# Table matmuls on TensorE ahead of five stages of a diffusion-transformer layer

## The chip, the cores and the metric

The kernel runs on one core of a Trainium2 chip. The metric is the device time of one execution in microseconds (us), median of several runs. The core's engines are TensorE (PE in the profile; its weight loads are PEld), VectorE (DVE), ScalarE (ACT), GpSimd (POOL) and SyncE (SP, which only issues transfers here).

## What is computed

The reference is one layer (depth 1, batch 1, 2048 latent tokens, 256 context tokens, width 1024, float32) of a hybrid backbone:

```python
h  = rmsnorm(x, norm1_w) * (1 + sc1) + sh1          # sc, sh, gt: silu(c) @ w_mod + b_mod
hc = rmsnorm(ctx, norm1_w) * (1 + csc1) + csh1
# mixer: p = h @ w_in, split into the inputs of three token mixers and 3 x 1024 gate columns
o_a = gdn_out(gdn_bidir(...))      # gated delta rule, 4 heads of 128, both directions, short conv, rotary
o_b = fourier_mix(ub)              # real part of a 2-D DFT over positions and channels
o_c = na_latent(...)               # neighbourhood attention on the latent grid plus context keys
y   = sigmoid(g_a)*(o_a @ w_br_a) + sigmoid(g_b)*(o_b @ w_br_b) + sigmoid(g_c)*(o_c @ w_br_c)
x   = x + gt1 * (y @ w_out)
h2  = rmsnorm(x, norm2_w) * (1 + sc2) + sh2
# 16 experts, each takes its 256 best tokens by router affinity (softmax, top_k)
hid = silu(xe @ w_gate) * (xe @ w_up)
x   = x + gt2 * scatter_add((hid @ w_down) * affinity)
```

## The kernel before

The program is a row of stages, each a function with its own SBUF and PSUM tensors, semaphores and one block of code for each engine: `delta_inputs` (modulation, norm, projection to q, k, v with conv, rotary and transposes), `mixer` (the other projections, Fourier mixing, attention), `delta_rule` (the chunked scan in both directions, written out as steps), `merge` (gates, branch projections, weighted sum), `project_out` (output projection, residual, second norm, router logits), `choose` (the top 256 tokens of each expert) and `experts`. Between two stages stands a barrier of all engines (`Scope.clear` and the end of a block): no engine issues an instruction of the next stage before all have ended the one before, last stores to DRAM included.

Within a stage each engine runs its own list in program order, and semaphores tie the lists together; there is no scheduler or planner. So a matmul stands where the code of TensorE's block puts it, and everything behind it on TensorE waits until it is issued.

Most of the large products are written as three matmuls of the type fp32r: each factor is split into a high part (rounded by ScalarE, `ACT.Copy` into an fp32r tensor) and a low part (the rest, subtracted by VectorE), and high x high, high x low and low x high are added up in PSUM. In `mixer` these are lines 913 to 915, in `merge` 2281 to 2283 (`product`), in `project_out` 2573 to 2575, in `experts` 2970, 2973 and 2987. TensorE can start on a weight tile only when VectorE has made its low part (`sb_wx_low` L1312, `sb_wm_low` L2430, `sb_yp_low` L2661, `sb_xe_parts` L3067). Other products are plain float32 matmuls, among them lines 965 to 968 and the sums of squares, which multiply by the constant table of ones (L2272 in `merge`), and transposes by the identity (L2959 in `experts`, L2584 in `project_out`).

The first work of TensorE behind each barrier that the change touches:

- `mixer`: `project`, 24 matmuls of 128x256 for one weight tile and 256 tokens (L913 to L915), the first one once `sb_wx_low` of weight tile 0 is there.
- `delta_rule`: `keys` and `scores` of both directions (L1780), which wait for the transfers of q and k, then `turn_m` (L1785), which waits for `sb_mt` (VectorE, from POOL's `sb_dq`, L1602).
- `merge`: for block 0, tile 0, `gate` 0 and `gate` 1 (24 matmuls of 128x512 each, whose operands were split in the stage before), then `sums` (4 float32 matmuls L2272 on squares of the two scans' sum, each answered by ACT L2332), then `gate` 2, whose weights ACT splits only behind the four roots L2332.
- `project_out`: `project(0, 0)`, 8 groups of 3 matmuls (L2573 to L2575), which waits for `sb_yp_low`.
- `experts`: `turn(0, 0)`, 16 transposes of the gathered tokens (L2959), then the gate and up products of expert 0.

The constant tables lie in the SBUF tensor `consts_sb`, float32: from column 0 on the identity, a table of ones, a block table and the rotary pairing, 128 columns each.

The functions that the diff touches:

Of the kernel before, what the change touches and what calls it, by code (L numbers as in the profile page):

```python
# [21 lines left out]
P = 128  # L22
# [623 lines left out]
def mixer(nc, g):  # L646
# [80 lines left out]
    with Scope(nc) as c:  # L727
# [15 lines left out]
        bank = psum(nc, c, "mix_ps", (P, 8, 512))  # L743
# [59 lines left out]
        with nc.Block() as block:  # L803
# [89 lines left out]
            def _(pe):  # L893
# [150 lines left out]
                    last.then_inc(sf.pq, 1)  # L1044

                item = 0
                for j, (_, ns) in enumerate(ALL):
                    if j >= NBA:
                        for a in range(CHB):
                            tokens(j, a)  # L1050
                    for t, n in enumerate(ns):
                        project(j, t, n)
                        if item:
                            norm_sum(item - 1)
                        if j >= NBA:
                            item += 1
# [359 lines left out]
def delta_rule(nc, g):  # L1416
# [15 lines left out]
    with Scope(nc) as c:  # L1432
# [66 lines left out]
        with nc.Block() as block:  # L1499
# [274 lines left out]
            def _(pe):  # L1774
# [124 lines left out]
                def step(n, u, old, new):  # L1899
# [74 lines left out]
                        turn_m(1, n + 1, v)  # L1974
                    known(1, n, u, every)
                    second(1, n, u, 6)
                for d in range(2):
                    keys(d, 0, 0, every)
                    scores(d, 0, 0, every)
                    turn_m(d, 0, 0)  # L1980
# [9 lines left out]
            def _(dve):  # L1990
# [116 lines left out]
                for d in range(2):  # L2107
                    matrix(d, 0, 0)
                    begin(d, 0, 0)
                    begin_turns(d, 0, 0)  # L2110
                walk(nc.vector, step)


def late_data(t, lev):
# [10 lines left out]
def merge(nc, g):  # L2125
# [11 lines left out]
    with Scope(nc) as c:  # L2137
# [53 lines left out]
        with nc.Block() as block:  # L2191
# [70 lines left out]
            def _(pe):  # L2262
# [23 lines left out]
                def block(b, more):  # L2286
                    def gate(m, br, first):
                        pe.wait_ge(s.wl, NC * m + br + 1 + WL0)
                        pe.wait_ge(s.sig, NBR * m + br + 1)
                        product(pg[br], br, (hh, hl), range(KD), s.hl if first and br == 0 else None, b).then_inc(s.gate, 1)  # L2290

                    def tile(m, u, first, near, last):
                        start = isinstance(m, int) and m == 0
                        ahead = first or near == 1
                        if ahead:

                            gate(m, 0, first)
                            gate(m, 1, first)
                            if start:
                                sums(0, range(H))  # L2300
                            gate(m, 2, first)
                        for br in order(m):
                            if not ahead:
                                gate(m, br, first)
                            if br == order(m)[0]:
                                pe.wait_ge(s.wl, NC * m + WB + 1 + WL0)
                            pe.wait_ge(s.prod, used(m, br))
                            product(pbr[br], WB, (oh, ol), range(*BRANCH[br]), s.ol if first else None, b).then_inc(s.br, 1)
                            if near == 0 and br < 2:
                                sums(b + 1, (2 * br, 2 * br + 1))  # L2310
                    tiles(nc.tensor, b, more, tile)
                blocks(nc.tensor, block)

            @block.scalar
# [173 lines left out]
def project_out(nc, g):  # L2488
# [4 lines left out]
    with Scope(nc) as c:  # L2493
# [32 lines left out]
        with nc.Block() as block:  # L2526
# [37 lines left out]
            def _(pe):  # L2564
# [31 lines left out]
                def step(t, u, more):  # L2596
# [3 lines left out]
                    project(t, u, 1, False)  # L2600
                    if not first(t):
                        turn(t - 1, 1 - u)
                steps(nc.tensor, step)
                route(LT - 2)
                turn(LT - 1, (LT - 1) % 2)
# [268 lines left out]
def experts(nc, g):  # L2874
# [9 lines left out]
    with Scope(nc) as c:  # L2884
# [17 lines left out]
        with nc.Block() as block:  # L2902
# [48 lines left out]
            def _(pe):  # L2951
# [10 lines left out]
                def expert(e, u, last_one):  # L2962
# [35 lines left out]
                    if last_one:  # L2998
                        last.then_inc(s.front, 1)
                        for f in range(NF):  # L3000
                            down(f, 1).then_inc(s.used, 1)
                turn(0, 0)
                with nc.tensor.Fori(0, E // 2 - 1) as i:
                    for u in range(2):
# [260 lines left out]
def program(nc, g, stages=99):  # L3265

    with Scope(nc) as c:
        consts = sbuf(nc, c, "consts_sb", [P, C_W])
        eps = sbuf(nc, c, "eps_sb", [P, 1])
        g.eps = eps[:]  # L3270
        g.ident, g.ones, g.blk, g.rot = (consts[:, at:at + P] for at in (C_ID, C_ONE, C_BLK, C_ROT))
        g.window = consts[:, C_WIN:C_WIN + GRID]
        g.flip = consts[:, C_FLIP:C_FLIP + P]
        g.dirt = lambda d, j: consts[:, C_DIR + (d * N_DIRT + j) * P:C_DIR + (d * N_DIRT + j + 1) * P]
# [58 lines left out]
```

## Time and profile before

| | |
|---|---|
| time, median of 3 runs | 3819.79 us (3817.61 to 3826.88) |
| span of the profiled execution, first to last instruction | 3823.5 us |
| its mean granted TensorE clock | 0.977 |
| TensorE busy | 3659.4 us, 96% of the span, 19520 matmul records |
| VectorE, ScalarE, GpSimd busy | 2323.0, 1645.7, 856.0 us |
| borders in the trace (us from the start) | mixer 551, delta rule 1157, merge 1661, output projection 2399, experts 2706 |

The profiled execution has no time of its own beside its span; its span lies 3.7 us above the median of the three timed runs and inside their range, so what lies around the span cannot be told from it. The granted clock is a share of TensorE's full 2.4 GHz; 0.50 is 1.2 GHz. A float32 matmul leaves two records in the trace, an fp32r one leaves one.

### The profile page before, as it was taken

Reading aid. Unit: us, or ns where it says so; the run is one execution under the profiler, and the core shown is the slowest. Engines: PE = TensorE matmul, PEld = TensorE weight load, DVE = VectorE, ACT = ScalarE, POOL = GpSimd, SP = SyncE. Lnnn points to the kernel's source line nnn. Section 1 sums busy time; section 2 is a strip of 40 time slices with the busy share of each in tenths; the row PEclk is TensorE's granted clock in tenths of the full one; section 3 lists DMA queues with packets and bytes.
Section 4 is the critical chain, followed back from the end, with each engine's and each line's share of the span. In section 5 each row is a group of like instructions: output and inputs, shape, how many; then the busy total and the mean of one; then the engine's idle time right before and its main releaser. Section 6 shows DMA issues by size and latency. Waiting matters only on the chain. (4 is left out here: it accounts for less than half of the span.)

```text
span 3823.5 us, 58042 instructions
## 1 busy us (share of the span) xinstructions
PE 3659.4 (96%) x19520; PEld 2936.9 (77%) x19520; DVE 2323.0 (61%) x3546; ACT 1645.7 (43%) x3006; POOL 856.0 (22%) x812
## 2 busy tenths in 40 slices
PE   8999999999997999989999999996799999999998
PEld 3444459986777999968888888785688888888887
DVE  4655632555656999953534353444767777677775
ACT  4333333334654666642424332322344445444452
POOL 3888500011106666610000000000000010000100
PEclk9999999999999999989999999997899999999999
DMA  7455455131115433344535352443477676766763
GB/s 283 155 144 142 119 182 130 57 86 45 26 46 183 125 118 122 96 160 125 177 105 170 99 172 73 152 154 130 145 214 226 214 220 206 214 224 215 219 209 92
DMA packets 258768, 570.97 MB, mean 149 GB/s; under 512 B 38971, under 2 KB 117339, under 8 KB 256347
## 3 DMA queue, kind: packets, MB, share of 16 engines
q1 hardware_dynamic: 225612, 451.18, 37.2%
q0 software_dynamic: 33040, 118.25, 10.4%
q8 instruction: 72, 1.18, 0.1%
q14 instruction: 44, 0.36, 0.0%
HBM read 458.27 MB, written 100.73 MB: 146 GB/s over the span
## 5 line engine op out<-in xcount | busy, mean ns | idle before, releaser
L3072 DVE TENSOR_TENSOR sb_we_low<-sb_we,sb_we_high 128x1024 fp32r<-128x1024 f32 x384 | 466.6, 1223 | 121.5 <-ACT sb_we_high L3023 121.5
L3023 ACT ACTIVATE sb_we_high<-sb_we 128x1024 fp32r<-128x1024 f32 x377 | 392.2, 1048 | 142.3 <-PE ey L2987 142.3
L2430 DVE TENSOR_TENSOR sb_wm_low<-sb_wm,sb_wm_high 128x1024 fp32r<-128x1024 f32 x127 | 155.4, 1224 | 393.6 <-ACT sb_wm_high L2340 393.6
L344 PE MATMUL p_ps<-sb_hT,sb_ring 128*128 128x512 f32 (+1 forms) x960 | 373.2, 549 | 0.0
L344 PEld LDWEIGHTS p_ps<-sb_hT,sb_ring 128*128 128x128 f32 x960 | 181.9, 190 | 186.2 <-issue 181.3
L2281 PE MATMUL pg<-sb_hb_high,sb_wm_high 128*128 128x512 f32 x768 | 303.3, 395 | 8.7 <-DVEq L2402 4.6
L2282 PE MATMUL pg<-sb_hb_low,sb_wm_high 128*128 128x512 f32 x768 | 300.4, 391 | 0.0
L2283 PE MATMUL pg<-sb_hb_high,sb_wm_low 128*128 128x512 f32 x768 | 300.1, 391 | 0.0
L2970 PE MATMUL eg<-sb_xe_parts,sb_we_high 128*128 128x512 f32 x1024 | 260.5, 396 | 1.6 <-DVE sb_xe_parts L3067 1.6
L2970 PE MATMUL eu<-sb_xe_parts,sb_we_high 128*128 128x512 f32 x1024 | 259.1, 395 | 0.0
L2932 POOL DMA_INDIRECT out<-sb_ybe,sb_ti x32 | 51.0, 1595 | 880.7 <-DVE sb_ybe L3107 822.7
L1997 DVE STREAM_TRANSPOSE sb_tm<-sb_um 64x128 f32<-64x128 f32 x720 | 219.8, 305 | 13.5
L2368 ACT ACTIVATE sb_sg<-pg 128x512 f32<-128x512 f32 x96 | 57.1, 595 | 396.3 <-PE pg L2283 396.2
L2970 PEld LDWEIGHTS eg<-sb_xe_parts,sb_we_high 128*128 128x128 f32 x1024 | 184.0, 188 | 37.4 <-issue 2.0
L2970 PEld LDWEIGHTS eu<-sb_xe_parts,sb_we_high 128*128 128x128 f32 x1024 | 182.9, 188 | 34.3
L3028 ACT ACTIVATE sb_sge<-sb_sge 128x256 f32<-128x256 f32 x128 | 53.5, 418 | 294.2 <-DVE sb_sge L3078 294.2
L1692 ACT ACTIVATE sb_pm<-dr_first 64x128 f32<-64x128 f32 x432 | 116.9, 271 | 141.0 <-PE dr_first L1798 134.8
L2281 PEld LDWEIGHTS pg<-sb_hb_high,sb_wm_high 128*128 128x128 f32 x768 | 145.0, 189 | 42.2 <-DVE sb_wm_low L2430 6.1
L3080 DVE TENSOR_REDUCE sb_sue<-eu 128x256 f32<-128x512 f32 x128 | 88.5, 692 | 144.8 <-PE eu L2973 143.9
L2282 PEld LDWEIGHTS pg<-sb_hb_low,sb_wm_high 128*128 128x128 f32 x768 | 145.1, 189 | 31.7 <-issue 1.4
L2283 PEld LDWEIGHTS pg<-sb_hb_high,sb_wm_low 128*128 128x128 f32 x768 | 145.2, 189 | 30.3
L2987 PE MATMUL ey<-sb_we_high,sb_hid_low 128*128 128x512 f32 x512 | 159.5, 393 | 0.0
(418 smaller groups left out, 8675.7 us busy)
## 6 DMA issues: line engine op xcount, KB each, us to landing
sb_we<-in_w_ex SPq DMA_DIRECT2D x384, 512.0 KB, 4.5
sb_wm<-in_w_gates SPq DMA_DIRECT2D x96, 512.0 KB, 3.6
sb_stage<-in_w_mod_row POOLq DMA_DIRECT2D x64, 256.0 KB, 3.6
sb_stage<-h_d SPq DMA_DIRECT2D x32, 512.0 KB, 4.3
sb_wm<-in_w_br SPq DMA_DIRECT2D x32, 512.0 KB
sb_ring<-in_w_ch POOLq DMA_DIRECT2D x19, 512.0 KB, 5.2
sb_gr<-gc_d SPq DMA_DIRECT2D x36, 256.0 KB, 3.8
sb_lk<-k_d SPq DMA_DIRECT2D x36, 256.0 KB, 4.0
```

The lines of the kernel that those rows point to most:

```text
L344: last = nc.tensor.matmul(ps[:, b % BANKS, 0:wd], w[:, kind, k], hT[:, k, t0:t0 + wd], start=(k == 0), stop=(k == KD - 1))
L1692: a(pm[d][rows, :, h], pairs(firsts[d])[rows, :, h], ACT.Copy).then_inc(q.pe, 1)
L1997: last = v.transpose(blocks(tm[d][u])[ROWS2[h], :, half], by_head(um[d][u])[ROWS2[half], :, h, half])
L2281: nc.tensor.matmul(bank[:], high, rh[:, k], start=(k == ks[0]), stop=False)
L2282: nc.tensor.matmul(bank[:], high, rl[:, k], start=False, stop=False)
L2283: last = nc.tensor.matmul(bank[:], low, rh[:, k], start=False, stop=(k == ks[-1]))
L2430: v.tensor_tensor(wl[n], w[n], wh[n], ALU.subtract).then_inc(s.wl, 1)
L2970: nc.tensor.matmul(bank[:], wh[:, n % CUT, k * P:(k + 1) * P], both, start=(k == 0), stop=False)
L2987: last = nc.tensor.matmul(py[a][q][:], lhs, rhs[:, n % CUT, q * 512:(q + 1) * 512], start=(f == 0 and lhs is high and rhs is wh), stop=(f ...
L3023: nc.scalar.activation(wh[:, n % CUT], w[:, n % RAW], ACT.Copy).then_inc(s.wh, 1)
L3072: v.tensor_tensor(wl[:, n % CUT], w[:, n % RAW], wh[:, n % CUT], ALU.subtract).then_inc(s.wl, 1)
L3080: v.tensor_reduce(su[:, f % 2], pu[f % 2][:].rearrange("p (a t) -> p t a", a=2), AX_X, ALU.add).then_inc(s.usum, 1)
```

## The change

A helper `keep_warm(nc, bank, tab, times)` issues float32 matmuls of `g.tables` (the first 512 columns of `consts_sb`; its first 128 columns, the identity, are the stationary side) into a PSUM bank that nothing reads before it is written anew. None of them waits for a semaphore or sets one. There are 35 of this size: 5 at the start of TensorE's block in `mixer`, 2 + 1 + 1 in `delta_rule`, 4 at the start of `merge`, 3 before and 2 behind its first `sums` (only for tile 0), 9 at the start of `project_out`, 9 at the start of `experts`. In `delta_rule` four matmuls of 64 rows and 512 columns (`firsts`, `seconds`) and eight of 128 rows, 64 output rows and 128 columns (`b_val`) stand between them. Nothing is removed, and no other engine's list changes.

```diff
--- before.py
+++ after.py
@@ -1044,6 +1044,7 @@
                     last.then_inc(sf.pq, 1)
 
                 item = 0
+                keep_warm(nc, bank[:, 4], g.tables, 5)
                 for j, (_, ns) in enumerate(ALL):
                     if j >= NBA:
                         for a in range(CHB):
@@ -1974,6 +1975,16 @@
                         turn_m(1, n + 1, v)
                     known(1, n, u, every)
                     second(1, n, u, 6)
+                half = slice(HALF, P)
+                keep_warm(nc, flat(b_state), g.tables, 2)
+                for _ in range(2):
+                    mm(flat(firsts[0]), g.tables[0:HALF, 0:P], g.tables[0:HALF, 0:512], start=True, stop=True)
+                    mm(flat(seconds[0]), g.tables[half, 0:P], g.tables[half, 0:512], start=True, stop=True)
+                keep_warm(nc, flat(b_state), g.tables, 1)
+                for _ in range(4):
+                    mm(flat(b_val)[0:HALF, 0:P], g.tables[:, 0:HALF], g.tables[:, 0:P], start=True, stop=True)
+                    mm(flat(b_val)[half, 0:P], g.tables[:, half], g.tables[:, P:2 * P], start=True, stop=True)
+                keep_warm(nc, flat(b_state), g.tables, 1)
                 for d in range(2):
                     keys(d, 0, 0, every)
                     scores(d, 0, 0, every)
@@ -2111,6 +2122,12 @@
                 walk(nc.vector, step)
 
 
+def keep_warm(nc, bank, tab, times):
+
+    for _ in range(times):
+        nc.tensor.matmul(bank, tab[:, 0:P], tab[:, 0:512], start=True, stop=True)
+
+
 def late_data(t, lev):
 
     return t.rearrange("p h (q z) -> p h q z", z=1 << lev)
@@ -2297,7 +2314,9 @@
                             gate(m, 0, first)
                             gate(m, 1, first)
                             if start:
+                                keep_warm(nc, pbr[0][:], g.tables, 3)
                                 sums(0, range(H))
+                                keep_warm(nc, pbr[1][:], g.tables, 2)
                             gate(m, 2, first)
                         for br in order(m):
                             if not ahead:
@@ -2309,6 +2328,7 @@
                             if near == 0 and br < 2:
                                 sums(b + 1, (2 * br, 2 * br + 1))
                     tiles(nc.tensor, b, more, tile)
+                keep_warm(nc, pbr[2][:], g.tables, 4)
                 blocks(nc.tensor, block)
 
             @block.scalar
@@ -2600,6 +2620,7 @@
                     project(t, u, 1, False)
                     if not first(t):
                         turn(t - 1, 1 - u)
+                keep_warm(nc, po[1][0][:], g.tables, 9)
                 steps(nc.tensor, step)
                 route(LT - 2)
                 turn(LT - 1, (LT - 1) % 2)
@@ -2999,6 +3020,7 @@
                         last.then_inc(s.front, 1)
                         for f in range(NF):
                             down(f, 1).then_inc(s.used, 1)
+                keep_warm(nc, pu[1][:], g.tables, 9)
                 turn(0, 0)
                 with nc.tensor.Fori(0, E // 2 - 1) as i:
                     for u in range(2):
@@ -3269,6 +3291,7 @@
         eps = sbuf(nc, c, "eps_sb", [P, 1])
         g.eps = eps[:]
         g.ident, g.ones, g.blk, g.rot = (consts[:, at:at + P] for at in (C_ID, C_ONE, C_BLK, C_ROT))
+        g.tables = consts[:, 0:512]
         g.window = consts[:, C_WIN:C_WIN + GRID]
         g.flip = consts[:, C_FLIP:C_FLIP + P]
         g.dirt = lambda d, j: consts[:, C_DIR + (d * N_DIRT + j) * P:C_DIR + (d * N_DIRT + j + 1) * P]
```

What moves on TensorE, in the program's order. At the start of `project_out` (`po00`, `po10` are PSUM banks of the output projection, `sb_wm0_high` and the like the split w_out, `sb_yp_high` the split rows), before:

```order
L2283 MATMUL pbr2<-sb_obr_high,sb_wm3_low 128x512
L2191 UNCONDITIONAL_BRANCH
L2563 UNCONDITIONAL_BRANCH [waits barrier_Pool_Activation_PE_DVE_SP_release]
L2573 MATMUL po00<-sb_wm0_high,sb_yp_high 128x512 [waits di_conv]
L2574 MATMUL po00<-sb_wm0_low,sb_yp_high 128x512
L2575 MATMUL po00<-sb_wm0_high,sb_yp_low 128x512
```

and now:

```order
L2300 MATMUL pbr2<-sb_obr_high,sb_wm3_low 128x512
L2208 UNCONDITIONAL_BRANCH
L2583 UNCONDITIONAL_BRANCH [waits barrier_Pool_Activation_PE_DVE_SP_release]
L2128 MATMUL po10<-sb_consts_sb 128x512 x9
L2593 MATMUL po00<-sb_wm0_high,sb_yp_high 128x512 [waits di_conv]
L2594 MATMUL po00<-sb_wm0_low,sb_yp_high 128x512
L2595 MATMUL po00<-sb_wm0_high,sb_yp_low 128x512
```

The nine stand behind the barrier's release and ahead of the first real matmul; they are in no other engine's way, but the real one is issued only after them. At the start of `merge` (`pg0`, `pbr2` are banks for a gate and for a branch), now:

```order
L1500 UNCONDITIONAL_BRANCH
L2278 UNCONDITIONAL_BRANCH [waits barrier_Pool_Activation_PE_DVE_SP_release]
L2128 MATMUL pbr2<-sb_consts_sb 128x512 x4
L2298 MATMUL pg0<-sb_hb_high,sb_wm0_high 128x512 [waits di_cdone,di_rot,di_proj]
L2299 MATMUL pg0<-sb_hb_low,sb_wm0_high 128x512
L2300 MATMUL pg0<-sb_hb_high,sb_wm0_low 128x512
```

Before, the first row behind the branch was the matmul into `pg0`; four table matmuls now stand ahead of it. Further on in `merge`, between gate 1 and gate 2 (`pnm` are the banks of the sums of squares), before:

```order
L2281 MATMUL pg1<-sb_hb_high,sb_wm1_high 128x512
L2282 MATMUL pg1<-sb_hb_low,sb_wm1_high 128x512
L2283 MATMUL pg1<-sb_hb_high,sb_wm1_low 128x512
L2272 MATMUL pnm0<-sb_prm,sb_consts_sb 128x512 [waits di_root]
L2272 MATMUL pnm1<-sb_prm,sb_consts_sb 128x512 [waits di_root]
L2272 MATMUL pnm0<-sb_prm,sb_consts_sb 128x512 [waits di_nrm,di_root]
L2272 MATMUL pnm1<-sb_yTb,sb_consts_sb 128x512 [waits di_nrm,di_root]
L2281 MATMUL pg2<-sb_hb_high,sb_wm2_high 128x512 [waits di_rot,di_proj]
L2282 MATMUL pg2<-sb_hb_low,sb_wm2_high 128x512
L2283 MATMUL pg2<-sb_hb_high,sb_wm2_low 128x512
```

and now:

```order
L2298 MATMUL pg1<-sb_hb_high,sb_wm1_high 128x512
L2299 MATMUL pg1<-sb_hb_low,sb_wm1_high 128x512
L2300 MATMUL pg1<-sb_hb_high,sb_wm1_low 128x512
L2128 MATMUL pbr0<-sb_consts_sb 128x512 x3
L2289 MATMUL pnm0<-sb_prm,sb_consts_sb 128x512 [waits di_root]
L2289 MATMUL pnm1<-sb_prm,sb_consts_sb 128x512 [waits di_root]
L2289 MATMUL pnm0<-sb_prm,sb_consts_sb 128x512 [waits di_nrm,di_root]
L2289 MATMUL pnm1<-sb_yTb,sb_consts_sb 128x512 [waits di_nrm,di_root]
L2128 MATMUL pbr1<-sb_consts_sb 128x512 x2
L2298 MATMUL pg2<-sb_hb_high,sb_wm2_high 128x512 [waits di_rot,di_proj]
L2299 MATMUL pg2<-sb_hb_low,sb_wm2_high 128x512
L2300 MATMUL pg2<-sb_hb_high,sb_wm2_low 128x512
```

Three table matmuls now stand between the last matmul of gate 1 and the first sum, and two between the last sum and gate 2.

## Rows read from the trace of the kernel before

**Rows 1.** Windows inside four stages: us, busy us (records) by engine, PEclk, DMA share, GB/s

```profile
570.00:780.00 210.00, 210.00 (x1697) 208.71 (x1695) 94.14 (x82) 81.12 (x168) 5.40 (x8) 1.00 0.36 95
1710.00:2385.00 675.00, 673.05 (x2945) 552.24 (x2944) 288.08 (x330) 236.70 (x298) 32.02 (x53) 1.00 0.42 137
2410.00:2610.00 200.00, 200.00 (x1047) 170.33 (x1045) 94.16 (x105) 53.92 (x101) 14.92 (x28) 1.00 0.41 144
2720.00:3790.00 1070.00, 1070.00 (x5793) 918.57 (x5792) 785.65 (x1037) 511.94 (x699) 77.61 (x59) 1.00 0.68 210
```

**Rows 2.** Windows at the five borders where the granted clock is 0.50, same columns

```profile
553.80:560.50 6.70, 5.97 (x28) 5.98 (x29) 4.17 (x4) 2.17 (x3) 1.59 (x3) 0.50 0.99 317
1158.00:1171.50 13.50, 4.42 (x19) 4.13 (x20) 1.35 (x4) 1.26 (x2) 9.39 (x14) 0.50 1.01 337
1659.80:1666.50 6.70, 4.68 (x11) 3.75 (x12) 0.00 (x0) 0.78 (x1) 2.96 (x4) 0.50 0.52 173
2397.00:2407.20 10.20, 6.06 (x14) 4.78 (x15) 7.34 (x7) 7.68 (x8) 0.00 (x0) 0.50 0.71 250
2704.20:2717.80 13.60, 3.65 (x16) 3.27 (x16) 10.11 (x15) 1.79 (x3) 3.07 (x2) 0.50 0.47 142
```

**Rows 3.** Timeline, float32 matmuls of 512 columns: start, us, engine, line, tiles, records

```profile
867.97 1.02 PE L966 MATMUL mix_ps<-sb_free,sb_ft 128*128 128x512 f32 x2
...
868.83 1.02 PE L967 MATMUL mix_ps<-sb_free,sb_ft 128*128 128x512 f32 x2
```

**Rows 4.** Timeline, start of the mixer, same columns, [idle before <-releaser]

```profile
551.02 1.06 ACT L1112 ACTIVATE sb_hx<-sb_stage 128x1024 fp32r<-128x1024 f32 x1 [1.85 <-PEq L122]
...
554.52 0.58 PE L913 MATMUL mix_ps<-sb_hx,sb_wx_high 128*128 128x256 f32 x1 [5.99 <-DVE sb_wx_low L1312]
...
559.81 0.41 PE L913 MATMUL mix_ps<-sb_hx,sb_wx_high 128*128 128x256 f32 x1
...
560.02 0.41 PE L914 MATMUL mix_ps<-sb_hx,sb_wx_high 128*128 128x256 f32 x1
...
561.71 0.28 PE L914 MATMUL mix_ps<-sb_hx,sb_wx_high 128*128 128x256 f32 x1
...
561.83 0.28 PE L915 MATMUL mix_ps<-sb_hx,sb_wx_low 128*128 128x256 f32 x1
```

**Rows 5.** Timeline, start of the delta rule

```profile
1166.59 2.08 PE L1780 MATMUL dr_key<-sb_lk 128*128 128x128 f32 x8 [12.62 <-DMA sb_lq<-q_d]
...
1169.05 1.04 POOL L1602 TENSOR_TENSOR sb_dq<-sb_dec,sb_beta 128x512 f32<-128x512 f32 x1
...
1170.86 0.98 PE L1785 MATMUL dr_key<-sb_consts_sb,sb_mt 128*128 128x128 f32 x4 [0.49 <-DVE sb_mt L2021]
```

**Rows 6.** Timeline, start of merge

```profile
1661.82 0.77 PE L2281 MATMUL pg<-sb_hb_high,sb_wm_high 128*128 128x512 f32 x1 [4.62 <-DVEq L2402]
...
1678.96 2.63 PE L2272 MATMUL pnm<-sb_prm,sb_consts_sb 128*128 128x512 f32 x4 [3.79 <-ACT sb_prm L2326]
...
1682.02 1.26 ACT L2332 ACTIVATE sb_of<-pnm,sb_eps_sb 128x512 f32<-128x512 f32 x2
...
1686.64 0.69 ACT L2332 ACTIVATE sb_of<-pnm,sb_eps_sb 128x512 f32<-128x512 f32 x1 [1.02 <-PE pnm L2272]
...
1703.61 0.50 PE L2281 MATMUL pg<-sb_hb_high,sb_wm_high 128*128 128x512 f32 x1 [1.10 <-DVE sb_wm_low L2430]
```

**Rows 7.** Timeline, start of the output projection

```profile
2398.78 1.06 ACT L2615 ACTIVATE sb_yp_high<-sb_zt 128x1024 fp32r<-128x1024 f32 x1 [7.67 <-PEq L122]
...
2401.14 0.79 PE L2573 MATMUL po<-sb_wm_high,sb_yp_high 128*128 128x512 f32 x1 [9.31 <-DVE sb_yp_low L2661]
```

**Rows 8.** Timeline, start of the experts

```profile
2705.71 0.24 DVE L3057 COPY sb_ti<-sb_top_idx 128x2 uint32<-128x2 uint32 x2 [1.29 <-PEq L122]
...
2714.15 3.67 PE L2959 MATMUL ey<-sb_consts_sb,sb_xe 128*128 128x128 f32 x16 [10.02 <-DMA sb_xe<-h_d,sb_ti]
...
2719.41 2.13 PE L2970 MATMUL eg<-sb_xe_parts,sb_we_high 128*128 128x512 f32 x8 [1.58 <-DVE sb_xe_parts L3067]
```

## Prediction, made before the changed kernel had run

> **What bounds the kernel now.** I read the page's busy times first: TensorE is busy for 3659.4 of 3823.5 us, and no other engine comes near. Then windows inside the stages [rows 1]: from 570 to 780 us, from 2410 to 2610 and from 2720 to 3790 it has no idle microsecond, from 1710 to 2385 it has two, all at a granted clock of 1.00. So inside mixer, merge, output projection and experts the end of the stage moves with TensorE, and whatever shifts its work at the start is kept to the end, later or earlier. Next I looked for stretches with a clock below 1.00. Nearly all lie at the borders, and five are those that the change aims at [rows 2]: 0.50, that is 1.2 GHz, for 6.7 to 13.6 us each, with 24.79 us of TensorE's busy time in them. Work at 1.2 GHz takes up to twice as long, so a perfect repair of all five is worth at most about 12 us. Last I read the timeline at each border for two times that the idle total hides: when the barrier lets the engines go, and when the first real operand is there. TensorE cannot begin on the tables before the release: the order shows them behind the branch that waits for it. Only the time between these two is free.
>
> **What one table matmul costs.** It is float32 with 512 columns. Such a matmul leaves two records, and at full clock the next starts 0.86 us later (867.97, 868.83) [rows 3]. I take 0.86 at 2.4 GHz and 1.71 at 1.2 GHz. All 35 are 30 us at full clock.
>
> The Trainium skill ("TensorE: Matmul & The Clock Gate", Back-to-back issue gap) gives 0.216 us for 512 columns at full clock; nine tables would be 1.9 us. That formula does not fit float32 operands, and rows 3 measure four times as much. "FP8 and Floating Point Precision", TensorE Precision Notes, says that true float32 takes four passes; by that the trace agrees.
>
> Do products of zeros and ones lift the clock at all? In [rows 8] the first work behind the last border is 16 transposes by the identity from 2714.15; the clock was 0.50 up to 2717.8 and is 1.00 afterwards [rows 2]. So I take a table as work like any other.
>
> **Mixer.** Release at 551.02, first operand at 554.52, TensorE idle since 548.53 [rows 4]: 3.5 us free. Five tables take 4.3 us and end at 555.3, 0.8 us late. The clock still stood at 1.00 at the release and fell by 553.8; with work from 551.0 on I take it that it stays up. The 28 records in the cold stretch stand 0.21 us apart (559.81, 560.02), at full clock 0.12 (561.71, 561.83): 28 x 0.09 = 2.5 us. Net -1.8 us. Bounds: if late weight tiles take it back, 0; if the clock falls anyway, 3.3 tables fit before 553.8 and the other 1.7 take 2.9 us, +2.2; if the lateness costs nothing, -2.5.
>
> **Delta rule.** Release at 1157 (the table's border), first operand (a transfer) at 1166.59 [rows 5]: 9.6 us free. Four wide tables are 3.4 us. No row shows matmuls on half the array; side by side the other twelve take 1.7 + 0.9 us, one after another 3.4 + 1.7: 6.0 to 8.5 us in all, and about 1.7 us more if the clock falls shortly after the release, which hides in the gap but for at most 0.7 us. The gain is small too: `turn_m` waits for POOL's `sb_dq`, which ends at 1170.09 whatever TensorE does; only its own 0.98 us shrinks to some 0.66. I take -0.3 us, bounds -1.5 and +1.5, since the clock may rise and fall elsewhere in the sparse first steps.
>
> **Merge.** Here the first operands are ready at the release: the first matmul at 1661.82 ends an idle time of 4.62 us that DVE's first semaphore of the block ends, not data [rows 6]. Four tables push everything behind them: cold until 1666.5 (4.7 us, 2.75 tables), the rest at full clock, end at 1667.6. By then TensorE had done 2.35 + 1.1 = 3.4 us worth of real work, so gates 0 and 1 end 3.4 us later. They ended at 1675.17, and TensorE then idled 3.79 us for `sb_prm`: the delay vanishes in that wait. The three tables behind gate 1 run from 1678.6 to 1681.2 and push the first sum from 1678.96; it ends at 1682.2 against ACT's roots 0 and 1, which ran from 1682.02, 0.2 us late. But TensorE no longer pauses, so the sums run at full clock. Sum 2 starts at about 1682.9 behind root 0 (0.63 us each), sum 3 follows at 1683.8 and ends at 1684.8; the last root then starts there instead of at 1686.64: -1.8 us. What hangs on it is the split of gate 2's weights and, through ACT and DVE in order, tile 1's weights, for which TensorE waits at 1703.61; that wait is a chain of splits and moves 1.8 us forward. The two tables behind the sums end before 1687. Net -1.8 us. Bounds: -3 with all cold work of this place regained, and +3.5 if the wait for `sb_prm` absorbs nothing.
>
> **Output projection.** Release at 2398.78, first operand at 2401.14 [rows 7]: 2.4 us free, at 0.50. Nine tables take 7.7 us at full clock. From 2398.7 they run cold; the clock rose 6 us after the work began in the mixer, 4.8 us in merge, 6.1 us here; I take 5.1, at 2403.8. That is 3.0 tables; the other six take 5.1 us, end at 2408.9. Before, real work from 2401.14 to 2407.2 at half speed was worth 3.0 us, and 1.7 us more until 2408.9: 4.7 us of real work that is now still to do. With no idle time until 2610 [rows 1] nothing hides it: +4.7 us. Bounds: +3.5 (clock back at once from 2400.4) and +8 (back only when all nine are cold for 8 us).
>
> **Experts.** Release at 2705.71, the gathered rows at 2714.15 [rows 8]: 8.4 us free, cold. Nine tables: cold until about 2711.0 (5.3 us, 3.1 tables), the rest 5.0 us: end 2716.0, 1.9 us late. The transposes then take at full clock about half of their 3.67 us and end at 2717.8, as before. The first product stood 1.6 us behind them (2719.41) while they set the pace of the splits on ACT and DVE; now the splits start later and set their own pace, for which I add 0.9 us, half of the lateness: +0.9 us. Bounds: -0.5 if the clock is back at once, +3 if it falls again while TensorE waits for the splits.
>
> **Sum.** -1.8 - 0.3 - 1.8 + 4.7 + 0.9 = +1.7 us on the profiled execution, from a span of 3823.5 to 3825.2. That span lies 3.7 us above the median of the timed runs and inside their range, so I put the difference on the median: 3819.79 + 1.7 = 3821.5 us. What differs from no change by under 0.3% (11.5 us) cannot be told from it here; the three runs before already span 9.3 us.
>
> **Rivals.** *The slip in the output projection is absorbed*, since VectorE still splits w_out while the tables run: then +4.7 goes and the time is 3816.8. Against it: TensorE is never idle behind 2410. 0.10.
>
> *The tables run cold to their end* (slower). The place is the last two borders, the price 1.71 us each: nine end at 2414.1, 13.0 us late, and in the experts at 2721.1, 6.9 us late; in merge four end at 1668.7, 3.1 us more than the wait absorbs, and three behind gate 1 add 2.6; the mixer adds 2.2. Together +27.8 us, 3848. It decides where the clock stays at 0.50 for more than the free time. For it: no row shows such a table matmul as the only work. Against: the transposes of rows 8. 0.05.
>
> *All tables hidden, all cold starts repaired* (faster): -12.4 us by rows 2, 3807.4. It would need the tables to run ahead of the release, in the idle time of 9.31 us that the row names. The order speaks against it. 0.04.
>
> *Cheap tables*: a quarter of the 0.86 us of rows 3, as if float32 took one record of 0.21 us. Then nothing is late; the mixer gives -2.5, merge -1.8, the projection at most about -1, the experts -0.5: -6, 3814. This is also where the skill's gap formula would lead. Rows 3 speak against it. 0.03.
>
> **How the numbers follow.** The forecast has 0.78. Its own range, from the terms' bounds and the spread of the runs, is 3815 to 3829; with the absorbed slip and some of the others 3813 to 3830. Slower by over 0.3%: the cold rival and a bad draw of the runs, 0.07. Faster by over 0.3%: 0.05. Same: 0.88.
>
> **What would show it.** In the new trace: nine tables on TensorE from about 2398.7 for some 10 us, the first real matmul of the projection near 2409 instead of 2401, and no less idle time behind it; in the experts the transposes up to 2 us late; in merge the sums at 1.00, the last root near 1685 and tile 1 near 1701.8; in the mixer a clock that does not fall. The stage lengths, release to release, should change by -1.8 (mixer), -0.3, -1.8, +4.7, +0.9. Wrong would be a first matmul at 2401 in spite of the tables, tables 0.21 us apart, or a change of over 8 us in any one stage.

## The result, and the profile after

| | before | after |
|---|---|---|
| time, median | 3819.66 us (3817.29 to 3826.88, 18 runs) | 3826.86 us (3822.15 to 3831.03, 18 runs) |
| span of the profiled execution | 3823.5 us | 3820.6 us |
| its mean granted clock | 0.977 | 0.982 |

The ratio is 1.0018, 95% interval 1.0011 to 1.0025: the change costs 4.2 to 9.6 us. That is within 0.3% and inside the forecast range of 3813 to 3830, but the forecast was +1.7 us and the median moved by +7.2. The two profiled executions differ the other way (-2.9 us). Where both are known, a time lies 1.5 us above the span of the same execution. So the profiled execution of after was a run of 3822.15 us, the fastest of its 18 and 4.7 us below their median. That of before would be some 3825.0 us, an estimate from the same 1.5 us, and 5.4 us above the median of its runs. A difference of a few us can't be read from one pair of profiles. The experiments add twelve more.

The five borders in the timeline of the changed kernel (start, us, engine, line, tiles, records, [idle before <-releaser]). The table matmuls are those of L2128. "PEq L122" is the barrier, and the row that it ends marks the release, the moment from which the engines may work on the stage:

```profile
550.07 1.06 ACT L1113 ACTIVATE sb_hx<-sb_stage 128x1024 fp32r<-128x1024 f32 x1 [1.85 <-PEq L122]
550.09 4.53 PE L2128 MATMUL mix_ps<-sb_consts_sb 128*128 128x512 f32 x10 [2.51 <-PEq L122]
...
554.05 0.68 PE L913 MATMUL mix_ps<-sb_hx,sb_wx_high 128*128 128x256 f32 x1
...
1153.38 3.53 PE L2128 MATMUL dr_state<-sb_consts_sb 128*128 128x512 f32 x4 [3.04 <-PEq L122]
...
1162.61 1.16 PE L1781 MATMUL dr_key<-sb_lk 128*128 128x128 f32 x8 [0.65 <-DMA sb_lq<-q_d]
...
1656.01 6.51 PE L2128 MATMUL pbr<-sb_consts_sb 128*128 128x512 f32 x8 [4.28 <-PEq L122]
1656.47 1.56 POOL L2228 DMA_DIRECT2D sb_of<-o_d  x2 [16.50 <-POOLq L122]
...
1673.25 2.73 PE L2128 MATMUL pbr<-sb_consts_sb 128*128 128x512 f32 x6
1675.82 2.99 PE L2289 MATMUL pnm<-sb_prm,sb_consts_sb 128*128 128x512 f32 x6
...
1679.71 0.69 ACT L2352 ACTIVATE sb_of<-pnm,sb_eps_sb 128x512 f32<-128x512 f32 x1 [0.17 <-PE pnm L2289]
...
2391.84 9.82 PE L2128 MATMUL po<-sb_consts_sb 128*128 128x512 f32 x18 [6.98 <-PEq L122]
2401.10 0.79 PE L2593 MATMUL po<-sb_wm_high,sb_yp_high 128*128 128x512 f32 x1
...
2704.55 7.96 PE L2128 MATMUL eu<-sb_consts_sb 128*128 128x512 f32 x18 [1.40 <-PEq L122]
...
2712.61 1.97 PE L2980 MATMUL ey<-sb_consts_sb,sb_xe 128*128 128x128 f32 x16
2716.65 2.12 PE L2991 MATMUL eg<-sb_xe_parts,sb_we_high 128*128 128x512 f32 x8 [2.07 <-DVE sb_xe_parts L3089]
```

- Mixer [rows 4]: the first real matmul (one that the result needs) stands 4.0 us behind the release, as five tables make it.
- Delta rule [rows 5]: the tables fit into the wait, the keys take 1.16 us instead of 2.08.
- Merge [rows 6]: the last of the four roots starts 23.2 us behind the release (1679.71 - 1656.47); before, 24.7 (1686.64 - 1661.94). So 1.5 us earlier; 1.8 were forecast.
- Output projection [rows 7]: the first real matmul is 9.3 us behind the release, before 2.4.
- Experts [rows 8]: the transposes run at full clock and end earlier, not later.

Windows of the same kernel at four of these places (us, busy us (records) of PE, PEld, DVE, ACT, POOL, granted clock, DMA share, GB/s), answering to [rows 2]:

```profile
552.00:562.00 10.00, 10.00 (x70) 8.56 (x69) 6.98 (x7) 6.01 (x7) 2.29 (x5) 1.00 0.96 312
...
1678.00:1690.00 12.00, 10.73 (x40) 7.15 (x39) 8.46 (x12) 8.85 (x12) 0.00 (x0) 1.00 0.26 87
...
2391.00:2402.00 11.00, 10.16 (x21) 4.68 (x22) 9.10 (x8) 7.69 (x8) 0.00 (x0) 0.79 0.82 286
2704.00:2712.00 8.00, 7.45 (x18) 3.34 (x18) 7.26 (x9) 0.00 (x0) 3.06 (x2) 1.00 0.45 133
```

At the mixer's and the experts' start the clock doesn't fall in this execution. At the projection's it is low for a part of the tables. So here the tables do to the clock what they were taken to do. The question is why the time doesn't follow.

One thing stood in none of the terms. At the end of the projection, from the last group of router matmuls (`plp`) to the next stage's first work, first before and then after:

```profile
2625.69 3.59 PE L2593 MATMUL plp<-sb_wr,sb_h2T 128*128 128x16 f32 x16 [0.69 <-ACT sb_h2T L2634]
...
2632.20 1.28 ACT L2753 ACT_TABLE_LOAD   x1 [2.70 <-PEq L122]
```

```profile
2623.13 3.59 PE L2613 MATMUL plp<-sb_wr,sb_h2T 128*128 128x16 f32 x16 [0.69 <-ACT sb_h2T L2655]
...
2631.60 1.28 ACT L2774 ACT_TABLE_LOAD   x1 [4.66 <-PEq L122]
```

From the first row to the second it is 6.51 us before and 8.47 after, with the same instructions between. ScalarE's wait for TensorE's sequencer at this barrier grew from 2.70 to 4.66 us. I call these 6.51 and 8.47 us the barrier behind the projection.

### The profile page after: what moved, and what is told of

Same layout as the page of the kernel before. It is cut to its first block and busy times, and to the rows that moved or that the text cites. A ratio compares the mean times of both kernels' runs of the same rounds, so it can differ in the third digit from the quotient of the medians.

```text
span 3820.6 us, 58234 instructions
## 1 busy us (share of the span) xinstructions
PE 3681.4 (96%) x19616; PEld 2941.1 (77%) x19616; DVE 2322.6 (61%) x3546; ACT 1646.5 (43%) x3006; POOL 855.8 (22%) x812
```

## The experiments

The kernel before was timed beside each of them, with medians of 3820.1 to 3820.5 us. "Wide" tables are the 512-column ones of the change, "narrow" ones have 8 columns and next to no work. Each kernel had 5 to 11 runs; the intervals say how little a difference of 1 to 3 us means.

| kernel | time, us | ratio to before, 95% interval |
|---|---|---|
| projection's tables alone | 3842.07 | 1.0041 to 1.0068 |
| merge's alone | 3834.62 | 1.0022 to 1.0049 |
| experts' alone | 3836.37 | 1.0026 to 1.0054 |
| all but the projection's | 3818.67 | 0.9987 to 1.0005 |
| projection's nine narrow | 3820.95 | 0.9995 to 1.0013 |
| all tables narrow | 3820.14 | 0.9992 to 1.0010 |
| before + 9 narrow | 3831.94 | 1.0021 to 1.0045 |
| before + 39 narrow | 3818.69 | 0.9989 to 1.0007 |
| before + 22 narrow | 3817.53 | 0.9987 to 1.0005 |
| projection's tables + 30 narrow | 3823.64 | 1.0000 to 1.0018 |
| five wide in the projection | 3823.94 | 0.9999 to 1.0017 |
| trimmed | 3818.56 | 0.9985 to 1.0003 |

**One border at a time.** In each of the first three only one border's tables are left of the change. The output projection's:

```diff
+                keep_warm(nc, po[1][0][:], g.tables, 9)
```

> Only the nine table matmuls at the start of the output projection are left; the other four places are as in the kernel before. T1 (the terms of the forecast hold, here as released-to-released length): +4.7 us, some 3824.4 us, and the first real matmul of the projection about 9 us behind the release. T2 (all of the measured +7 us is made here, through a longer stage or a later end that the forecast sized too small): +7 to +10 us, 3827 to 3830. T3 (the slip is absorbed before the stage ends): 0 to +1 us, 3820. In the profile of the changed kernel this stage, release to release, was 6.4 us longer, so I lean between T1 and T2: +6.

3842.07 us, +21.6. All three theories (T1 to T3) missed by far. Merge's tables alone:

```diff
+                                keep_warm(nc, pbr[0][:], g.tables, 3)
                                 sums(0, range(H))
+                                keep_warm(nc, pbr[1][:], g.tables, 2)
...
+                keep_warm(nc, pbr[2][:], g.tables, 4)
```

> Only the tables of merge are left: four at its start, three ahead of the first sums, two behind them. T1: -1.8 us (the sums run at full clock, the last root starts earlier), 3818.0 us. T3 (the four tables push real work that nothing hides, or the cold time comes back elsewhere): +1 to +3 us. The last root L2352 behind the release: 20.4 us with the tables, 24.7 us in the kernel before. That distance tells whether the mechanism works; the time tells whether it lasts.

3834.62 us, +14.1, although the merge stage itself was 735.2 us, shorter than the 736.8 of before. The last root started 23.1 us behind the release, 1.6 us earlier than before; the 20.4 us of the expectation are missed (in the changed kernel the first of the four roots stands there). The experts' tables alone:

```diff
+                keep_warm(nc, pu[1][:], g.tables, 9)
```

> Only the nine tables at the start of the experts are left. T1 (forecast): +0.9 us, 3820.7 us, the transposes up to 2 us late. By the stage length read in the profile of the changed kernel: -1.9 us, 3817.9. T3 (the clock falls again behind the tables, or the nine run longer in most executions): +2 to +3 us, 3822 to 3823.

3836.37 us, +15.9. And with all but the projection's:

```diff
-                keep_warm(nc, po[1][0][:], g.tables, 9)
```

> All table matmuls but the nine of the output projection. T1 (forecast terms: -1.8 mixer, -0.3 delta rule, -1.8 merge, +0.9 experts): -3.0 us, 3816.7 us. By the stage lengths read in the profile of the changed kernel (-2.7, -1.8, -1.5, -1.9) it would be -7.9 us, 3812. T2 (the loss is all in the output projection): 0 to -3 us. T3 (the loss sits in several places, which gain nothing on average over executions): +1 to +4 us, 3821 to 3824. With only_project it should add up to the whole change, +7 us.

3818.67 us, -1.8, with an interval that includes no change. That fits T1, but the parts don't add up: +21.6 for the projection's tables alone and -1.8 for all others make 20, and the whole change made 7.2. The releases of the stages say where it is: from the experts' release to the end the three single ones take 1135.4, 1132.4 and 1132.9 us, before 1117.8, after 1115.9, all but the projection's 1116.6. A window inside the experts, of before, and then of the kernel with the projection's tables alone:

```profile
2850.00:3690.00 840.00, 840.00 (x4538) 720.68 (x4537) 615.44 (x813) 401.05 (x546) 66.66 (x51) 1.00 0.70 215
```

```profile
2850.00:3690.00 840.00, 829.15 (x4446) 708.36 (x4445) 603.51 (x796) 394.95 (x536) 63.53 (x48) 1.00 0.69 213
```

Same clock, 92 matmul records fewer in 840 us (2%, some 17 us). The waits of TensorE in that kernel (line, releaser: us, times, longest), and one place of its timeline:

```profile
PE eg L2980 <- issue: 7.3, 5, 2.0
PE eg L2977 <- issue: 3.4, 5, 1.1
```

```profile
2997.80 2.12 PE L2977 MATMUL eg<-sb_xe_parts,sb_we_high 128*128 128x512 f32 x8 [0.61 <-issue]
...
3002.19 0.84 PE L2980 MATMUL eg<-sb_xe_parts,sb_we_low 128*128 128x256 f32 x5 [1.91 <-issue]
```

"issue" means that TensorE waited for nothing that the profile shows. The same pair stands at 2856.79 and 2861.23, 141 us before. One of the two or both stand at six places, one for each branch back of the experts' loop (seven rounds). The two lines add up to 10.7 us; the rest of the 17 us stands in no wait. And the queue that carries code (packets, MB, share), of before and then of that kernel:

```profile
q8 instruction: 72, 1.18, 0.1%
```

```profile
q8 instruction: 126, 2.06, 0.2%
```

Some 16 KB each. 126 packets stand in all three single ones, 72 or 73 in before, after and all but the projection's. I read this as code of the loop that is fetched anew in each round, or stays. The three slow kernels have the same 36 instructions more than before, four for each of nine tables (58078 in all, before 58042), all of them ahead of the loop. So the place of the loop's code may be what tells them from the others: 0 instructions further, it stays; 36, it doesn't; 156 and 192, it stays. I call this T4.

The Trainium skill ("Runtime: NRT & Kernel Launch", Instruction fetch mechanics) says that TensorE's instruction memory has 128 KiB, 2048 instructions, is refilled in blocks of 16 KiB (256 instructions), and that a taken branch whose target "isn't in the current 2-page window" forces a fetch before execution goes on. The packets of 16 KB and the waits behind the branch agree. The window of two pages doesn't: by the kernel's text a round has 768 matmul records and as many weight loads, and before ran seven rounds of that with 72 packets and no wait for issue.

The 54 packets more, over six branches back, are nine for each. By the page's sizes nine blocks are one more than its 2048 instructions. This gives an estimate of why the place can decide: the 1536 matmuls and weight loads of a round fill six blocks, and semaphore waits and register instructions come on top. If all together take up almost eight blocks, the loop touches eight or nine of them, according to where it begins. No run counts the loop's instructions, so this stays an estimate; the next kernels test the place itself.

**Place without work.** The next kernels use a table matmul of 8 columns:

```diff
+def narrow(nc, bank, tab, times):
+    for _ in range(times):
+        nc.tensor.matmul(bank[:, 0:8], tab[:, 0:P], tab[:, 0:8], start=True, stop=True)
```

To the kernel before, nine of them at the start of the delta rule are added:

```diff
+                narrow(nc, flat(b_state), g.tables, 9)
                 for d in range(2):
                     keys(d, 0, 0, every)
```

> The kernel before with nine table matmuls of 8 columns at the start of the delta rule, where TensorE waits 9.6 us for a transfer: hardly any work, all hidden, but everything behind stands 36 instructions later in TensorE's list, as in the kernels that kept nine tables at a single place. T1 (work and clock): 0 us. T4 (place of the code): +14 to +18 us, all of it in the experts' loop, with waits for issue of about 2 us in each round of the loop and about 126 instruction packets on q8 instead of 72.

3831.94 us, +11.8 (1.0021 to 1.0045), 126 packets, and in the loop:

```profile
PE eg L2986 <- issue: 5.5, 5, 2.0
PE eg L2983 <- issue: 2.4, 5, 0.7
```

Nine matmuls of next to no work, in a wait of TensorE, cost 12 us, which work and clock (T1) can't explain. The 14 to 18 us expected were a little too many. Then 20 there and 19 at the start of the experts:

```diff
+                narrow(nc, flat(b_state), g.tables, 20)
...
+                narrow(nc, pu[1][:], g.tables, 19)
```

> As before, but 20 such matmuls of 8 columns at the start of the delta rule and 19 at the start of the experts, both in waits for transfers: the experts' loop stands 156 instructions later in TensorE's list, the distance that the kernel without the projection's tables had. T4 (the place of the loop in the code, not the number of instructions, decides): no waits for issue in the loop, about 73 instruction packets on q8, 0 to +2 us against the kernel before. If it is the number of instructions that costs: over +15 us.

3818.69 us, -1.4, 73 packets, no wait for issue, and the window of before again:

```profile
2850.00:3690.00 840.00, 840.00 (x4546) 721.08 (x4545) 617.16 (x817) 401.14 (x547) 68.33 (x52) 1.00 0.70 216
```

Thirty-nine cost nothing, nine cost 12 us. And with 22 (`narrow(nc, flat(b_state), g.tables, 22)` at the same place):

> As the kernel with nine narrow matmuls at the start of the delta rule, but 22 of them: a distance of 88 instructions, between 36 (loop refetches its code, 126 packets) and 156 (it doesn't, 73). Either outcome fits T4 and places its edge: 126 packets and 3832 us, or 73 and 3819 to 3820. 150 packets or a value in between would speak against a place that simply fits or doesn't.

3817.53 us, -2.6, 73 packets: an edge lies between 36 and 88 instructions (another one between 0 and 36). The slow kernels, repaired by more instructions:

```diff
+                narrow(nc, flat(b_state), g.tables, 20)
...
+                keep_warm(nc, po[1][0][:], g.tables, 9)
...
+                narrow(nc, pu[1][:], g.tables, 10)
```

> The kernel that has only the nine wide tables of the output projection (3842.1 us, of which some 17 us in the experts' loop), with 30 matmuls of 8 columns more: 20 at the start of the delta rule, 10 at the start of the experts, in waits. That brings the experts' loop to a distance of 156 instructions, as in the kernels whose loop never waited for code. T4 (place of the code): 73 instruction packets, no waits for issue in the loop, an experts stage of 1117 to 1119 us, and of the loss only the work in the projection is left, 231.3 us from its release to the last router matmuls: 3824 to 3826 us, 16 us faster by adding instructions. Rival (the tables of the projection themselves slow the loop): over 3838.

3823.64 us, 18.4 below the same kernel without the 30. The experts stage took 1116.9 us, without a wait for issue, and the code queue shows

```profile
q8 instruction: 73, 1.20, 0.1%
```

T4 holds. What is left is the price of the projection's nine tables in timed runs, free of the loop: 3.6 us against the kernel before (interval 0 to 6.9), 5 to 6 us against the two padded kernels without wide tables (3818.69, 3817.53).

**The projection in the changed kernel.** Its nine tables made narrow, all else as changed:

```diff
-                keep_warm(nc, po[1][0][:], g.tables, 9)
+                narrow(nc, po[1][0][:], g.tables, 9)
```

> The changed kernel, but the nine table matmuls of the output projection multiply 8 columns instead of 512; their number and place in TensorE's list stay. T1 (their work is what costs there): the release to the start of the last router matmuls goes from 231.3 us back to about 227, the whole from +7.2 to about +2.5 us against the kernel before, 3822. T4 (the place in the list costs too: the 2.0 us more between the last router matmul and the next stage, 4.84 instead of 2.88 us in the changed kernel, comes from the code that TensorE had still to fetch): that 4.8 us stays although the work is gone. Without T4 it falls to 2.9 us.

3820.95 us, 5.9 below the changed kernel. The release to the last router matmuls is 228.1 us where about 227 were expected, the barrier behind them 7.6 us: of the 2.0 us more, a part stayed without the work. With five wide:

```diff
-                keep_warm(nc, po[1][0][:], g.tables, 9)
+                keep_warm(nc, po[1][0][:], g.tables, 5)
+                narrow(nc, po[1][0][:], g.tables, 4)
```

> The changed kernel, but of the nine tables of the output projection five are wide and four have 8 columns; the number of instructions stays. By the arithmetic of the forecast: three run cold in 5.1 us, two take 0.86 us each, and the real work starts some 3 us earlier than behind nine. Release to the last router matmuls 231.3 - 4 x 0.86 + about 0.6 = 228.5 us; the whole 2.8 us below the changed kernel, 3824. The 1 to 2 us behind the last router matmuls stay, as the place stays.

3823.94 us, 2.9 below where 2.8 were expected. That is weak support: its eleven runs spread over 9 us, and the profiled execution had 230.0 us where 228.5 were expected. The barrier took 8.0 us. With all tables at all places narrow (`keep_warm` to `narrow`, and 512 and 128 columns to 8 in the delta rule's own):

> The changed kernel with every table matmul cut to 8 columns, at all places. So TensorE's list has the length of the changed kernel's, with next to none of its work and warm-up. T1 (only the work and the clock count): the gains of mixer, merge and experts go, the loss of the projection goes, 0 us against the kernel before, with stage lengths of 606, 505, 737, 233.4 and 1117.8 us. T4 (the place of the code counts): the same, and +2.0 us behind the projection's last matmul; 3821 to 3822.

3820.14 us, 0.0; barrier 7.3 us. The end of the projection stands 156 instructions further than before in exactly four kernels: the changed one and these three. They have 8.5, 7.6, 8.0 and 7.3 us there. The other ten, at 0 to 120, all have 6.51 to 6.54. So this goes with the place too, 0.8 to 2.0 us, and not with the tables' work. No packet count or wait for code shows how; in the time of the last kernel it can't be seen (3821 to 3822 were expected with it, 3820 without), and why it varies is open.

**A version that could beat both.** No tables in the projection, and fewer in the mixer and the experts, so that they end before the first operand at full clock; delta rule and merge as changed:

```diff
-                keep_warm(nc, bank[:, 4], g.tables, 5)
+                keep_warm(nc, bank[:, 4], g.tables, 4)
+                narrow(nc, bank[:, 4], g.tables, 1)
...
-                keep_warm(nc, po[1][0][:], g.tables, 9)
...
-                keep_warm(nc, pu[1][:], g.tables, 9)
+                keep_warm(nc, pu[1][:], g.tables, 5)
+                narrow(nc, pu[1][:], g.tables, 4)
```

> A version that could beat both: no tables in the output projection; four wide and one narrow in the mixer (3.5 us are free there), five wide and four narrow in the experts (8.4 us are free), delta rule and merge as changed. The experts' loop keeps its distance of 156 instructions, the end of the projection one of 120, at which the barrier took 6.5 us. Expected: -2 to -5 us against the kernel before, 3815 to 3818; the experts stage about 1116, the mixer 603, merge 735.3, the projection 226.3 to the last router matmuls. Rival (the borders' gains are smaller than the spread of the low clock elsewhere): 0 to -2.

3818.56 us, -1.5, interval 0.9985 to 1.0003: the rival's case. The 22 narrow matmuls that warm nothing have a median 1 us lower. The four other borders have no gain that can be told from none.

## Why the prediction was right and where it was wrong

The stage lengths of all 14 profiled executions, each from release to release, in us: mean (lowest to highest, number). Wide means at least four wide tables at that border, and in the row of the barrier a place 156 instructions further; the projection's three kernels with narrow or five tables are left out, the experts' four with refetched code too.

| stage | wide tables | no wide tables | difference | forecast |
|---|---|---|---|---|
| mixer | 603.1 (602.1 to 604.3, 5) | 603.4 (602.1 to 606.1, 9) | -0.3 | -1.8 |
| delta rule | 503.1 (502.7 to 503.4, 5) | 504.0 (502.5 to 505.0, 9) | -0.9 | -0.3 |
| merge | 735.1 (734.5 to 735.4, 6) | 736.0 (734.6 to 736.9, 8) | -0.9 | -1.8 |
| projection to its last router matmuls | 231.4 (231.3 to 231.8, 3) | 226.5 (226.2 to 226.9, 8) | +5.0 | +4.7 |
| barrier behind them (at 156, else) | 7.8 (7.3 to 8.5, 4) | 6.5 (6.51 to 6.54, 10) | +1.3 | none |
| experts | 1117.8 (1115.9 to 1119.9, 5) | 1117.9 (1116.9 to 1119.6, 5) | -0.1 | +0.9 |

They add up to +4.1 us, or to +4.8 with the 2.0 us that the changed kernel's own barrier took; measured are 4.2 to 9.6. Some 2.4 to 3.1 us of the median's 7.2 have no place in this table. Only the projection and the barrier stand clear of their spread; in the other rows the ranges overlap. Stretches that the change doesn't touch vary as much: from the start to the mixer's release it is 550.1 to 553.8 us in the 14 executions, and between the barrier and the experts 72.3 to 73.5.

- **Bound and mechanism: right.** The tables begin behind the release, 0.86 us each at full clock (nine took 7.96 us in the experts), and what is late in the projection is never caught up. The rivals "cheap tables", "all hidden" and "cold to their end" fall with the projection's first real matmul at 9.3 us behind the release; "slip absorbed" falls with the 5.0 us that its stage is longer.
- **Projection: right, +4.7 forecast, +5.0 in the profiles, 3.6 to 6 in the times.** The clock came back earlier than assumed and the first real matmul 0.8 us earlier, but the stage lost what was said.
- **Missing term: the barrier behind the projection, +2.0 in the changed kernel, +1.3 in the mean.** "Nothing is removed, and no other engine's list changes" was read as: nothing else can move. But 156 instructions move the place of all code behind them.
- **Mixer: mis-sized, -1.8 forecast, -0.3 measured.** The cold start was repaired in part, and [rows 4] were one execution. Of the nine kernels without wide tables seven need 602.1 to 603.7 us with the same cold start, and two, before among them, 606. What these two have is a clock that falls twice more in the middle of the stage. The same two stretches, of before, and of the kernel with 22 narrow ones:

```profile
857.50:861.00 3.50, 3.50 (x5) 1.51 (x5) 1.99 (x1) 0.60 (x1) 3.12 (x2) 0.51 0.06 22
874.50:878.00 3.50, 3.50 (x5) 1.51 (x5) 0.00 (x0) 0.60 (x1) 1.29 (x2) 0.52 0.36 143
```

```profile
857.50:861.00 3.50, 3.50 (x10) 1.48 (x8) 1.54 (x2) 0.12 (x1) 2.32 (x2) 1.00 0.07 29
874.50:878.00 3.50, 3.50 (x9) 1.27 (x8) 2.05 (x4) 0.14 (x1) 0.00 (x0) 1.00 0.32 125
```

  The kernel before with this clock would be some 3 us faster in its profile. Of the -2.7 us between the mixers of the first pair, 1.5 are there 284 us behind the release, where L965 begins (283.6 us in the changed kernel, 285.1 in before): that is the start. The rest comes later, where the changed kernel has one such fall less; it has one at 862.93:

```profile
862.93 2.04 PE L965 MATMUL mix_ps<-sb_free,sb_ft 128*128 128x512 f32 x2
...
864.76 1.85 PE L966 MATMUL mix_ps<-sb_free,sb_ft 128*128 128x512 f32 x2
```

  Up to L965 the nine kernels without wide tables already vary from 284.1 to 285.1 us: 16 us behind the release they have 82 to 90 records of real matmuls behind them, the changed kernel 96. So the price of the cold start varies too, and before was among those that paid most. And the tables don't hold the clock in every execution: in three of the five kernels that have them here, five took 4.53 us; in the other two the clock fell under them, as in the one with five wide in the projection:

```profile
553.78 6.23 PE L2128 MATMUL mix_ps<-sb_consts_sb 128*128 128x512 f32 x10 [2.51 <-PEq L122]
559.45 0.68 PE L913 MATMUL mix_ps<-sb_hx,sb_wx_high 128*128 128x256 f32 x1
```

  Its first real matmul stands 5.7 us behind the release instead of 4.0. That was the forecast's bound "if the clock falls anyway". So the mean at L965 is 284.2 us with tables and 284.7 without: the step that was mis-sized is the start itself, 0.5 us instead of 1.8.

- **Merge: right in its steps, half the size.** The four tables put the first real matmul 5.9 us behind the release, and the wait for `sb_prm` takes that up; sums at full clock, last root 1.5 us earlier (1.8 forecast), in the stage mean 0.9.
- **Delta rule: within its bounds**, -0.9 instead of -0.3.
- **Experts: wrong in its first step, small in the sum.** "Cold until about 2711.0" did not happen in the changed kernel: the clock was at 1.00 at the release and the nine took 7.96 us. In the kernel with the experts' tables alone they took 10.64 us. Whether this border goes cold varies from execution to execution, and the stage follows it. With nine wide tables it took 1115.9 and 1116.6 us in the two executions whose nine took 7.96 us, 1118.9 where they took 9.66 and 1119.9 where they took 10.68.
- **The sum** put five terms of 0.3 to 4.7 us on one execution. It missed the median by 5.5 us. The two gains of 1.8 us were larger than measured (together 2.4 us too much), and 1.3 to 2.0 us stood at a barrier that had no term; delta rule and experts came out 1.6 us better than said. Net, that accounts for 2.4 to 3.1 of the 5.5 us; the rest is open. The forecast range of 17 us held all of this.

No rival of mine had the place of the code in it, and its price in the experts' loop is up to 18 us, more than the whole range. The changed kernel escaped it because its 36 wide tables (not 35, as the texts ahead count them) and twelve others, four instructions each, come to 192 and not to 36. That was luck, in the change and in the forecast.

## What to carry to other kernels

Instructions that do nothing for the result still take room in their engine's code. Where that engine runs a long loop, compare the instruction queue's packets and the waits for "issue" before and after any edit ahead of the loop, and undo an edit together with its room (same number of instructions, less work), or the experiment measures the loop instead of the edit. Warm an engine only between the release and its first operand. What stands behind that point is paid where the engine is never idle again, less what the warmer clock gives back: the projection's tables made the first real matmul 6.9 us late and the stage 5.0 us longer.

## What the runs showed of the hardware

- When the code of the experts' loop stood 36 instructions later, the instruction queue carried 126 packets of 16 KB instead of 72 or 73, nine more for each of six branches back; at 0, 88, 156 and 192 it didn't. The stage took 12 to 18 us more than 1118, with waits of up to 2.1 us at the start of a round.
- The barrier behind the projection took 7.3 to 8.5 us instead of 6.5 in the four kernels whose code stood 156 instructions later there.
- A float32 matmul of 128x512 takes 0.86 us at full clock and 1.71 at 1.2 GHz (two in 3.42 us from 2391.84) also when it is a table with zeros and ones. With nothing else on the engine the clock rose under the projection's tables: 0.50 up to 2395.0, 1.00 from 2396.0, and the first real matmul stands at 2401.10.
- The clock can fall to 0.51 in the middle of a stage with TensorE busy all the time (before at 857.5 to 861), in some executions and not in others, and costs some 1.7 us each time. Behind a barrier it can fall while table matmuls run, too: five took 6.23 us in one execution and 4.53 in three.
